# Gate-up weights of a mixture of experts: two quarter loads of 16 KB runs against one half load of 32 KB runs

## The chip, the cores and the metric

The kernel runs on one core of a Trainium2 chip. The metric is the device time of one execution in microseconds. The kernel before takes 1092.41 us, the median of three runs (1090.91 to 1093.58).

## The reference

One step of a decoder layer for 256 prompt tokens, with 16 meta tokens ahead of them, and 8 sample tokens. A mixer comes first; then a mixture of experts takes most of the time:

```
logits = xt @ w_router + b_router;  top_val, top_idx = lax.top_k(logits, 4);  gates = softmax(top_val)
for each expert e of 32, on the tokens that chose it:
    hgu  = x @ w_gu[e] + b_gu[e]                       # 1024 x 2048 weights, float32: 8.39 MB
    gate = minimum(hgu[:, :1024], 7);  up = clip(hgu[:, 1024:], -7, 7)
    act  = gate * sigmoid(1.702 * gate) * (up + 1)
    y   += (act @ w_down[e] + b_down[e]) * gate_of_token   # 1024 x 1024 weights: 4.19 MB
```

So each expert needs 12.58 MB of float32 weights from HBM, and 32 experts need 403 MB of the 432.68 MB that the whole kernel moves.

## The kernel before

The program is written engine by engine: each engine has one list of instructions, and semaphores join them. `sp` (SyncE) issues the weight loads, `pe` (TensorE) multiplies, `act` and `v` (ScalarE and VectorE) do what lies between. Nothing is reordered by a scheduler.

An *item* is one expert with 64 slots for its tokens. (If an expert had more than 64 tokens, further rounds of 32 items would follow; `more` is their number, and in this profile there are none.) TensorE does for item i:

1. `gate_up(i)`: eight steps k = 0 to 7, each with one slot of `gu_ring` as the moving operand (128 rows of w_gu, 2048 columns, four products of 512 columns). Each step adds 1 to `gu_used`. After k = 2, 4 and 6 stands one `scatter` of item i-2 (L1122, L1124), which brings its result back to the tokens. Items 28, 29 and 30 each have one scatter with bias products besides (L1119).
2. `way_back(i-1)` (L1157, L1159), then `gather()` for item i+1 (L1078), 56 small products.
3. `down(i-1)` (L1175): eight steps over `down_ring`; every second one adds 1 to `down_used`.
4. `turn(i)` (L1189, L1193): transposes of the hidden values.

`gu_ring` has 16 slots of 8 KB a partition: two items of eight slots, by parity. `down_ring` has eight slots of 4 KB a partition: one item, two halves. Of w_gu, `load_gu(e, parity, m)` brings a *chunk* m of 256 rows (0 to 3), 2.1 MB, into two slots: partition p gets rows 2p and 2p+1 of the chunk, one run of 16 KB. Each chunk has its own semaphore, `gu_landed[4 * parity + m]`, and TensorE waits for it at k = 0, 2, 4, 6 (L1142). `load_down` brings a half of w_down, also 2.1 MB in runs of 16 KB. `load_row` brings one slot of the first experts in runs of 8 KB.

All of these loads stand in one queue, in the order in which SyncE issues them, and SyncE waits before each until its slots are free: chunk m of item i after `gu_used` = 8i + 2m - 14 (step k = 2m + 1 of item i-2), half h of down(i) after `down_used` = 4i + 2h - 2. The order has three stages:

- *first stage*, to item 9: gate-up of i+2, then down of i;
- *middle stage*: chunks 2 and 3 of gate-up i+1, chunks 0 and 1 of gate-up i+2, then down of i;
- *last stage*, from down of 20 on: gate-up of i+1, then down of i. The last down weights (item 31) are loaded into free slots of `gu_ring` behind everything else.

The hidden index of the tokens' values has to be dealt to partitions as the rows of w_gu are. So the transposes and the gather read columns with a step of 2 (`(p r)` with r=2, L882, L989, L1079), and the router's weights are loaded likewise.

Of the kernel before, what the change touches and what calls it, by code (L numbers as in the profile page):

```python
# [51 lines left out]
def build(nc, x_prompt, x_sample, state_pool, state_conv, meta_tokens, g_mix, w_in, w_pool_grp, pool_scale,  # L52
          w_pool_up, w_conv, w_conv_out, w_o, g_ffn, w_router, b_router, w_gu, b_gu, w_down, b_down, g_final,
          y_prompt, y_sample, new_pool_prompt, new_conv_prompt, new_pool_sample, new_conv_sample):
    with ExitStack() as ctx:
# [108 lines left out]
        gffn_rows = low[0:CH, 9856:9856 + 2 * P]  # L164
# [143 lines left out]
        gu_landed = [sem(f"gu_landed{s}") for s in range(KT)]  # L308
        beside_landed = sem("beside_landed")
# [60 lines left out]
        def _(sp):  # L370
# [3 lines left out]
            def load_rows():  # L374
                for c in range(CH):
                    sp.dma_start(bgu_rows[E * c:E * c + E, :], b_gu[0, :, HALF * c:HALF * c + HALF]
                                 ).then_inc(rows_landed, 16)
                sp.dma_start(pool_rows, state_pool[0].rearrange("b r d -> (b r) d")).then_inc(rows_landed, 16)
                sp.dma_start(conv_rows, state_conv[0].rearrange("b r d -> (b r) d")).then_inc(rows_landed, 16)
                sp.dma_start(param_rows[0:4, :], pool_scale[0].rearrange("(k p) -> k p", p=P)).then_inc(rows_landed, 16)  # L380
                sp.dma_start(param_rows[4:16, :], w_conv[0].rearrange("w (k p) -> (w k) p", p=P)
                             ).then_inc(rows_landed, 16)
                sp.dma_start(gffn_rows, g_ffn[0].rearrange("(m c) -> m c", c=2 * P)).then_inc(rows_landed, 16)
# [28 lines left out]
            def load_row(e, parity, k):  # L412
                m, r = divmod(k, 2)
                sp.dma_start(gu_ring[:, KT * parity + k, :],
                             w_gu[0, e, 2 * P * m:2 * P * m + 2 * P, :].rearrange("(p r) n -> p r n", r=2)[:, r, :]
                             ).then_inc(gu_landed[CH * parity + m], 16)

            def load_gu(e, parity, m):
                src = w_gu[0, bass.ds(e, 1), 2 * P * m:2 * P * m + 2 * P, :].rearrange("a (p r) n -> (a p) (r n)", r=2)
                sp.dma_start(gu_ring[:, KT * parity + 2 * m:KT * parity + 2 * m + 2, :].rearrange("p s n -> p (s n)"),  # L420
                             src).then_inc(gu_landed[CH * parity + m], 16)
# [45 lines left out]
            def item_gu(i, e, parity, chunks=range(CH)):  # L467
                for m in chunks:
                    sp.wait_ge(gu_used, 8 * i + (2 * m - 14))
                    load_gu(e, parity, m)  # L470


            for k in range(2):
                sp.wait_ge(gu_used, k + 1)
                load_row(2, 0, k)
            item_gu(2, 2, 0, (1, 2, 3))
            item_gu(3, 3, 1)
# [15 lines left out]
            first, second = (0, 1), (2, 3)  # L493
# [18 lines left out]
            with sp.Fori(0, E // 2 - 2 - AHEAD - HALVED) as pair:  # L512
# [11 lines left out]
            with sp.If(more > 0):  # L524
                with sp.Fori(0, more) as r:
                    with sp.Fori(0, E // 2) as pair:
                        e0 = sp.snap(2 * pair)
                        e1 = sp.snap(2 * pair + 1)
                        e_before = sp.snap((2 * pair + (E - 1)) % E)
                        before = sp.snap(r * E + 2 * pair + (E - 1))  # L530
                        item_down(before, e_before)
                        item_gu(before + 1, e0, 0)
                        item_down(before + 1, e0)
                        item_gu(before + 2, e1, 1)
# [46 lines left out]
        def _(act):  # L581
# [67 lines left out]
            for b in range(NCHUNK // 2):  # L649
# [15 lines left out]
                if b == 4:  # L665
                    act.dma_start(wr[:].rearrange("p (m r) e -> p m r e", r=2),
                                  w_router[0].rearrange("(m p r) e -> p m r e", p=P, r=2)).then_inc(late_landed, 16)
# [187 lines left out]
        def _(pe):  # L855
# [23 lines left out]
            def turn_small_rows():  # L879
                pe.wait_ge(rows_landed, 144)  # L880
                nc.tensor.transpose(PS[:, 4, 8:24], param_rows, ident[0:16, 0:16])
                by_r = gffn_rows.rearrange("m (p r) -> m r p", r=2)  # L882
                for q in range(2):
                    last = nc.tensor.transpose(PS[:, 4, 24:32].rearrange("p (m r) -> p r m", r=2)[:, q, :], by_r[:, q, :],
                                               ident[0:CH, 0:CH])
# [101 lines left out]
            def by_row(rows, t, k):  # L987
                m, q = divmod(k, 2)
                return Y[0:rows, t, 2 * P * m:2 * P * m + 2 * P].rearrange("t (p r) -> t r p", r=2)[:, q, :]  # L989
# [85 lines left out]
            def gather_parts(k, parts, first, final, rows=None):  # L1075
                m, q = divmod(k, 2)
# [56 lines left out]
            def gate_up(i, u, landed, two_before, bias=None):  # L1133
# [62 lines left out]
            def item(i, u, landed, before=None, two_before=None, bias=None):  # L1196
                gate_up(i, u, landed, two_before, bias)
# [8 lines left out]
            gate_up(0, 0, 32, None)  # L1206
# [5 lines left out]
            item(1, 1, 32, 0)  # L1212
# [3 lines left out]
            with pe.Fori(0, more * (E // 2) + (E // 2 - 3)) as pair:  # L1216
                item(2 * pair + 2, 0, 16 * pair + 48, 2 * pair + 1, 2 * pair)
                item(2 * pair + 3, 1, 16 * pair + 48, 2 * pair + 2, 2 * pair + 1)
# [5 lines left out]
            landed = more * (8 * E) + (8 * E + 16)  # L1224
            pe.wait_ge(gt_kept, NT + 1)
            pe.wait_ge(late_landed, 80)
            item(from_end(4), 0, more * (8 * E) + 8 * E, from_end(5), from_end(6), bias=0)
            item(two_before, 1, more * (8 * E) + 8 * E, from_end(4), from_end(5), bias=1)
            item(before, 0, landed, two_before, from_end(4), bias=2)

            gate_up(last, 1, landed, two_before)
# [489 lines left out]
```

## Time and profile before

| | |
|---|---|
| median of three runs | 1092.41 us |
| profiled execution, device time | 1091.76 us |
| its span, first to last instruction | 1090.0 us |
| TensorE busy | 1050.4 us, 96% |
| VectorE / ScalarE busy | 458.7 / 173.6 us |
| moved by DMA | 432.68 MB, mean 397 GB/s |
| granted TensorE clock, mean | 0.998 of full |

TensorE and the DMA engines are both busy for nearly the whole span. A share of busy time cannot tell which of the two sets the end. The views to read are the transfer rate by stretch, and in each stage which wait TensorE ends last. The DMA share of a stretch can read slightly over 1, since packets of one engine overlap a little.

### The profile page before, as it was taken

The page shows a single profiled execution, that of the slowest core. Times are in us where ns is not written, and L with a number is a line of the kernel's source. Part 1 is how long each engine was busy: PE and PEld are TensorE (multiplying, and loading weights), DVE is VectorE, ACT ScalarE, POOL GpSimd, SP SyncE. Part 2 cuts the span into 40 slices and gives each one's busy share as a digit, 9 for nine tenths or more (in the row PEclk, how much of TensorE's full clock was granted, in tenths as well). Part 3 has the DMA queues.
Part 4 walks back from the last instruction along what each step waited for, and adds up shares of the span by engine and source line. Part 5 has one row for each costly group of instructions (what it writes and reads, how often), then busy time and mean ns, then how long its engine had stood idle before and what let it go on. Part 6 is the DMA issues. An engine that isn't in the chain of part 4 may idle for free.

```text
span 1090.0 us, 17300 instructions
## 1 busy us (share of the span) xinstructions
PE 1050.4 (96%) x7080; PEld 510.9 (47%) x7081; DVE 458.7 (42%) x776; ACT 173.6 (16%) x293; POOL 8.9 (1%) x21
## 2 busy tenths in 40 slices
PE   8999999999999999999999999999999999999995
PEld 7999975433344333444333333333433333343332
DVE  5677665333333333333333333333333333333344
ACT  5445533100000000000000000000000000000012
POOL 1000100000000000000000000000000000000000
PEclk9999999999999999999999999999999999999999
DMA  9972899999999999999999999999999999999993
GB/s 299 289 231 95 335 407 376 428 429 425 429 427 430 426 431 426 430 427 429 429 427 430 427 430 426 431 426 430 427 429 428 428 430 427 429 426 427 427 424 146
DMA packets 52482, 432.68 MB, mean 397 GB/s; under 512 B 4630, under 2 KB 21546, under 8 KB 26205
## 3 DMA queue, kind: packets, MB, share of 16 engines
q1 hardware_dynamic: 50959, 431.04, 95.2%
q10 hardware_dynamic: 1494, 1.22, 0.4%
q8 instruction: 22, 0.36, 0.1%
q14 instruction: 7, 0.06, 0.0%
HBM read 431.10 MB, written 1.39 MB: 397 GB/s over the span
## 4 chain that ended last, share of the span: by engine, by line
PE 61%; DMA 30%; DVE 4%; issue 4%; ACT 1%; SPq 1%; DVEq 0%; ACTq 0%
PE PS L1146 22%; DMA down_ring<-in_w_down_dram 19%; PE PS L1175 16%; DMA gu_ring<-in_w_gu_dram 11%; PE PS L914 9%; PE PS L1078 3%; PE PS L1122 2%; PE PS L945 2%; PE PS L1124 1%; PE PS L1189 1%; PE PS L1159 1%; PE PS L1157 1%; DVE pick_twice L1582 1%; PE PS L1193 1%; PE PS L865 0%
## 5 line engine op out<-in xcount | busy, mean ns | idle before, releaser
L1146 PE MATMUL PS<-gu_ring,XgT 128*64 128x512 f32 x2048 | 469.0, 599 | 4.0 <-DMA gu_ring<-in_w_gu_dram 4.0
L1146 PEld LDWEIGHTS PS<-gu_ring,XgT 128*64 128x64 f32 x2048 | 135.1, 136 | 267.2 <-issue 247.1
L1175 PE MATMUL PS<-down_ring,actT 128*64 128x512 f32 x984 | 219.7, 596 | 9.8 <-DMA down_ring<-in_w_down_dram 9.8
L1613 DVE TENSOR_TENSOR Y<-PS,Y 128x1024 f32<-128x1024 f32 (+1 forms) x96 | 117.0, 1220 | 255.1 <-PE PS L1124 255.1
L1175 PEld LDWEIGHTS PS<-down_ring,actT 128*64 128x64 f32 x984 | 67.3, 137 | 137.6 <-issue 118.4
L1644 DVE SCALAR_TENSOR_TENSOR y_low<-PS,slot_gate,y_high 128x512 fp32r<-128x512 f32 x31 | 23.3, 751 | 231.7 <-ACT y_high L801 231.7
L813 ACT ACTIVATE work<-PS 128x512 f32<-128x512 f32 x32 | 19.1, 597 | 456.3 <-PE PS L1146 456.3
L914 PE MATMUL PS<-h_high,win_high 128*128 128x264 f32 (+2 forms) x256 | 71.2, 287 | 0.0
L914 PE MATMUL PS<-h_high,win_low 128*128 128x264 f32 (+2 forms) x256 | 71.0, 286 | 0.0
L914 PE MATMUL PS<-h_low,win_high 128*128 128x264 f32 (+2 forms) x256 | 70.9, 286 | 0.0
L801 ACT ACTIVATE y_high<-PS,slot_gate 128x512 fp32r<-128x512 f32 x31 | 21.3, 687 | 258.4 <-PE PS L1175 258.4
L1078 PE MATMUL PS<-pick,XP 128*128 128x64 bf16 x1768 | 56.7, 193 | 0.0
L1078 PEld LDWEIGHTS PS<-pick,XP 128*128 128x128 bf16 x1768 | 56.2, 99 | 0.0
L1122 PEld LDWEIGHTS PS<-y_high,spread 64*128 64x128 f32 x186 | 17.3, 183 | 75.3 <-issue 74.5
L914 PEld LDWEIGHTS PS<-h_high,win_high 128*128 128x128 f32 x256 | 47.4, 189 | 0.4 <-issue 0.2
L914 PEld LDWEIGHTS PS<-h_low,win_high 128*128 128x128 f32 x256 | 47.4, 188 | 0.3 <-DVE h_low L1308 0.2
L914 PEld LDWEIGHTS PS<-h_high,win_low 128*128 128x128 f32 x256 | 47.3, 188 | 0.1
L1303 DVE TENSOR_TENSOR win_low<-gu_ring,win_high 128x2048 fp32r<-128x2048 f32 x15 | 34.4, 2292 | 30.2 <-ACT win_high L616 30.2
L1122 PE MATMUL PS<-y_high,spread 64*128 64x512 f32 x186 | 46.6, 498 | 0.0
L1550 DVE TENSOR_TENSOR XgT<-PS,params 128x512 f32<-128x512 f32 x31 | 21.4, 692 | 55.3 <-PE PS L1078 55.3
L1621 DVE TENSOR_TENSOR work<-PS,bias_gu 128x512 f32<-128x512 f32 x64 | 44.0, 687 | 1.2 <-PE PS L1193 0.6
L1124 PE MATMUL PS<-y_low,spread 64*128 64x512 f32 x186 | 36.7, 391 | 0.0
(235 smaller groups left out, 775.9 us busy)
## 6 DMA issues: line engine op xcount, KB each, us to landing
gu_ring<-in_w_gu_dram SPq DMA_DIRECT2D x119, 2048.0 KB, 28.2
down_ring<-in_w_down_dram SPq DMA_DIRECT2D x60, 2048.0 KB, 21.9
gu_ring<-in_w_gu_dram SPq DMA_DIRECT2D x18, 1024.0 KB, 9.4
gu_ring<-in_w_in_dram SPq DMA_DIRECT2D x16, 1024.0 KB, 9.5
gu_ring<-in_w_down_dram SPq DMA_DIRECT2D x4, 1024.0 KB, 27.9
down_ring<-in_w_down_dram SPq DMA_DIRECT2D x3, 1024.0 KB, 9.4
down_ring<-in_w_pool_up_dram SPq DMA_DIRECT2D x1, 2048.0 KB, 11.5
gu_ring<-in_w_conv_out_dram SPq DMA_DIRECT2D x2, 1024.0 KB, 6.2
```

Of the source, the lines that this page charges most:

```text
L914: return mm(PS[:, n % 4, 0:COLS - lo], w[:, k, P * (n % 2):P * (n % 2) + P], h[:, k, lo:COLS], start=first, stop=final)
L945: last = mm(PS[:, 4 + n % 4, 0:TOK], of(w, k, m), x[:, k, :], start=(k == 0 and part == 0), stop=(k == CH - 1 and part == 2))
L1078: last = mm(rows if rows is not None else PS[:, 5, SLOTS * k:SLOTS * k + SLOTS], XP[:, part, 2 * P * m:2 * P * m + 2 * P].rearrange("t (p ...
L1122: mm(PS[:, bank + h, :], way[rows, t, :], y_high[rows, :], start=not bias, stop=False)
L1124: last = mm(PS[:, bank + h, :], way[rows, t, :], y_low[rows, :], start=False, stop=True)
L1146: last = mm(PS[SLOTS * h:SLOTS * h + SLOTS, b, :], XgT[:, k, :], w[:, D * b + HALF * h:D * b + HALF * h + HALF], start=(k == 0), stop=(k = ...
L1175: last = mm(PS[SLOTS * h:SLOTS * h + SLOTS, bank, :], acts[:, f % 4, f // 4, :], rows[:, f, HALF * h:HALF * h + HALF], start=(f == 0), sto ...
L1303: tt(win_low[:, b % WIN_SLOTS, :], gu_ring[:, b % WIN_SLOTS, :], win_high[:, b % 2, :].bitcast(F32), ALU.subtract).then_inc(win_ready, 1)
L1550: tt(XgT[:], PS[:, 5, :].rearrange("p (k s) -> p k s", k=KT), g_ffn_cols.unsqueeze(2).to_broadcast([P, KT, SLOTS]), ALU.mult).then_inc(xg_ ...
L1613: tt(Y[rows, t, :].rearrange("p (h n) -> p h n", h=2), PS[rows, bank:bank + 2, :], Y[rows, t, :].rearrange("p (h n) -> p h n", h=2), ALU.a ...
L1621: tt(hgu[:, HALF * b:HALF * b + HALF].rearrange("p (c s) -> p c s", s=SLOTS), PS[:, 2 + b, :].rearrange("p (c s) -> p c s", s=SLOTS), bias ...
L1644: stt(y_low[:], PS[:, bank, :], gate[:], y_high[:].bitcast(F32), ALU.mult, ALU.subtract).then_inc(low_ready, 1)
```

## The change

The gate-up weights of experts 4 to 29, and the second half of expert 3, are loaded by halves of 512 rows, 4.2 MB each: partition p gets rows 4p to 4p+3 of the half, one run of 32 KB. There are 53 such half loads in place of 106 chunk loads. Experts 30 and 31, all but the last half of experts 2 and 3, stay in chunks: a chunk is now two of the four rows of each partition, a run of 16 KB with a step of 32 KB between partitions. TensorE waits twice in an item instead of four times (k = 0 and k = 4), SyncE issues a half when all four slots of it are free (`gu_used` = 8i + 4h - 12). The first waits of items 2 and 3 have semaphores of their own. Everything that is dealt as the rows are has a step of 4 instead of 2. The order of the loads by item stays; the last two items are written out behind the test for further rounds.

```diff
+            def load_gu(e, parity, m, signal):
+                h, q = divmod(m, 2)
+                src = w_gu[0, bass.ds(e, 1), HALF * h:HALF * h + HALF, :].rearrange("a (p q r) n -> (a p) q (r n)", q=2, r=2)
                 sp.dma_start(gu_ring[:, KT * parity + 2 * m:KT * parity + 2 * m + 2, :].rearrange("p s n -> p (s n)"),
-                             src).then_inc(gu_landed[CH * parity + m], 16)
+                             src[:, q, :]).then_inc(signal, 16)
+
+            def load_half(e, parity, h):
+                src = w_gu[0, bass.ds(e, 1), HALF * h:HALF * h + HALF, :].rearrange("a (p r) n -> (a p) (r n)", r=CH)
+                at = KT * parity + CH * h
+                sp.dma_start(gu_ring[:, at:at + CH, :].rearrange("p s n -> p (s n)"), src
+                             ).then_inc(half_landed[2 * parity + h], 16)
...
-            def item_gu(i, e, parity, chunks=range(CH)):
-                for m in chunks:
-                    sp.wait_ge(gu_used, 8 * i + (2 * m - 14))
-                    load_gu(e, parity, m)
+            def item_gu(i, e, parity, halves=range(2)):
+                for h in halves:
+                    sp.wait_ge(gu_used, 8 * i + (4 * h - 12))
+                    load_half(e, parity, h)
...
-            item_gu(2, 2, 0, (1, 2, 3))
-            item_gu(3, 3, 1)
+            for m, signal in ((1, half_landed[0]), (2, third_chunk), (3, half_landed[1])):
+                item_chunk(2, 2, 0, m, signal)
+            for m, signal in ((0, fourth_chunk), (1, half_landed[2])):
+                item_chunk(3, 3, 1, m, signal)
+            item_gu(3, 3, 1, (1,))
...
-            with sp.Fori(0, E // 2 - 2 - AHEAD - HALVED) as pair:
+            with sp.Fori(0, E // 2 - 3 - AHEAD - HALVED) as pair:
...
+            for u in range(2):
+                for m in range(CH):
+                    item_chunk(more * E + (E - 2 + u), E - 2 + u, u, m, gu_landed[CH * u + m])
+                item_down(more * E + (E - 3 + u), E - 3 + u)
...
             def gather_parts(k, parts, first, final, rows=None):
-                m, q = divmod(k, 2)
+                m, q = divmod(k, CH)
                 for n, (part, t) in enumerate(parts):
                     last = mm(rows if rows is not None else PS[:, 5, SLOTS * k:SLOTS * k + SLOTS],
-                              XP[:, part, 2 * P * m:2 * P * m + 2 * P].rearrange("t (p r) -> t r p", r=2)[:, q, :],
+                              XP[:, part, HALF * m:HALF * m + HALF].rearrange("t (p r) -> t r p", r=CH)[:, q, :],
...
-                    if k % 2 == 0:
-                        by_row = 16 if k == 0 and u == 0 and two_before is not None else 0
-                        pe.wait_ge(gu_landed[CH * u + k // 2], landed + by_row)
+                    if chunks and k % 2 == 0:
+                        pe.wait_ge(gu_landed[CH * u + k // 2], landed)
+                    elif not chunks and k % CH == 0:
+                        if k == 0:
+                            pe.wait_ge(*((fourth_chunk, 16) if u else (third_rows, 32)))
+                        elif u == 0:
+                            pe.wait_ge(third_chunk, 16)
+                        pe.wait_ge(half_landed[2 * u + k // CH], landed)
...
-            item(before, 0, landed, two_before, from_end(4), bias=2)
-
-            gate_up(last, 1, landed, two_before)
+            item(before, 0, 48, two_before, from_end(4), bias=2, chunks=True)
+
+            gate_up(last, 1, 48, two_before, chunks=True)
```

What moves on TensorE is shown at the gate-up of an odd item inside the loop over pairs of items, where the last stage has its waits. One step k is four products here, at L1146 (after: L1174); in the trace each product is two records, so a step is eight. Before:

```order
L1146 MATMUL PS<-gu_ring,XgT 64x512 [waits gu_landed4,xg_ready]
L1146 MATMUL PS<-gu_ring,XgT 64x512 x7
L1146 MATMUL PS<-gu_ring,XgT 64x512 [waits gu_landed5]
L1146 MATMUL PS<-gu_ring,XgT 64x512 x3
L1130 ISA [waits low_ready]
L1122 MATMUL PS<-y_high,spread 128x512 [waits added]
L1122 MATMUL PS<-y_high,spread 128x512
L1124 MATMUL PS<-y_low,spread 128x512 x2
L1146 MATMUL PS<-gu_ring,XgT 64x512 x4
L1146 MATMUL PS<-gu_ring,XgT 64x512 [waits gu_landed6]
```

After, at the same place:

```order
L1174 MATMUL PS<-gu_ring,XgT 64x512 [waits half_landed2,fourth_chunk,xg_ready]
L1174 MATMUL PS<-gu_ring,XgT 64x512 x11
L1153 ISA [waits low_ready]
L1145 MATMUL PS<-y_high,spread 128x512 [waits added]
L1145 MATMUL PS<-y_high,spread 128x512
L1147 MATMUL PS<-y_low,spread 128x512 x2
L1174 MATMUL PS<-gu_ring,XgT 64x512 x4
L1174 MATMUL PS<-gu_ring,XgT 64x512 [waits half_landed3]
```

The products and their order are the same; the wait ahead of k = 2 is gone, what it waited for now stands ahead of k = 0, and the wait ahead of k = 4 asks for chunks 2 and 3 together.

On SyncE, the loop of the last stage (L512; after: L530), one item of it. Before:

```order
L420 ISA [waits gu_used]
L420 DMA gu_ring<-in_w_gu_dram 128x4096
L469 REGISTER_ALU
L420 ISA [waits gu_used]
L420 DMA gu_ring<-in_w_gu_dram 128x4096
L464 ISA
L427 ISA [waits down_used]
L427 DMA down_ring<-in_w_down_dram 128x4096
L427 ISA [waits down_used]
L427 DMA down_ring<-in_w_down_dram 128x4096
```

These are chunks 2 and 3 of an item's gate-up load and both halves of its down load. After:

```order
L431 ISA [waits gu_used]
L431 DMA gu_ring<-in_w_gu_dram 128x8192
L480 REGISTER_ALU
L431 ISA [waits gu_used]
L431 DMA gu_ring<-in_w_gu_dram 128x8192
L475 ISA
L438 ISA [waits down_used]
L438 DMA down_ring<-in_w_down_dram 128x4096
L438 ISA [waits down_used]
L438 DMA down_ring<-in_w_down_dram 128x4096
```

Here the two gate-up rows are the whole item: four chunk loads of 4096 values a partition have become two loads of 8192 values, ahead of the same two down loads.

## Rows read from the trace of the kernel before

**Rows 1.** Page, part 2: 40 slices of the span (27.25 us each).
```profile
PE   8999999999999999999999999999999999999995
DMA  9972899999999999999999999999999999999993
GB/s 299 289 231 95 335 407 376 428 429 425 429 427 430 426 431 426 430 427 429 429 427 430 427 430 426 431 426 430 427 429 428 428 430 427 429 426 427 427 424 146
```

**Rows 2.** Busy time by window: length; PE, PEld, DVE, ACT, POOL; clock; DMA; GB/s.
```profile
131.00:143.00 12.00, 12.00 (x119) 9.14 (x118) 6.33 (x26) 3.76 (x7) 4.07 (x6) 1.00 1.00 410
134.00:154.00 20.00, 20.00 (x145) 15.12 (x145) 13.88 (x26) 4.39 (x13) 2.41 (x4) 1.00 1.02 421
570.00:780.00 210.00, 199.71 (x1305) 79.55 (x1303) 73.70 (x120) 17.95 (x36) 0.00 (x0) 1.00 1.01 429
```

**Rows 3.** TensorE in time, item 3 (first stage): start, length, line, idle before it.
```profile
243.66 5.37 PE L1146 MATMUL PS<-gu_ring,XgT 128*64 128x512 f32 x24
...
249.63 3.65 PE L1146 MATMUL PS<-gu_ring,XgT 128*64 128x512 f32 x16
...
271.26 5.37 PE L1146 MATMUL PS<-gu_ring,XgT 128*64 128x512 f32 x24
```

**Rows 4.** TensorE in time, middle stage, two items.
```profile
630.07 3.65 PE L1175 MATMUL PS<-down_ring,actT 128*64 128x512 f32 x16 [1.24 <-DMA down_ring<-in_w_down_dram]
...
659.44 3.65 PE L1175 MATMUL PS<-down_ring,actT 128*64 128x512 f32 x16 [1.24 <-DMA down_ring<-in_w_down_dram]
...
664.18 5.37 PE L1146 MATMUL PS<-gu_ring,XgT 128*64 128x512 f32 x24
```

**Rows 5.** TensorE in time, last stage, the gate-up of item 26 and the next.
```profile
894.36 1.94 PE L1146 MATMUL PS<-gu_ring,XgT 128*64 128x512 f32 x8 [0.25 <-DMA gu_ring<-in_w_gu_dram]
...
899.25 1.94 PE L1146 MATMUL PS<-gu_ring,XgT 128*64 128x512 f32 x8 [0.43 <-DMA gu_ring<-in_w_gu_dram]
...
904.15 1.94 PE L1146 MATMUL PS<-gu_ring,XgT 128*64 128x512 f32 x8 [0.44 <-DMA gu_ring<-in_w_gu_dram]
...
919.82 3.65 PE L1146 MATMUL PS<-gu_ring,XgT 128*64 128x512 f32 x16
```

**Rows 6.** The chain that ended last, two transfers of it: start, length.
```profile
950.16 37.13 DMA gu_ring<-in_w_gu_dram
...
1010.73 41.73 DMA gu_ring<-in_w_gu_dram
```

**Rows 7.** TensorE in time, items 29 to 31 and the last down.
```profile
989.21 1.98 PE L1119 MATMUL PS<-Y,work 32*128 32x512 f32 x4
...
1009.16 5.37 PE L1146 MATMUL PS<-gu_ring,XgT 128*64 128x512 f32 x24
...
1019.37 1.94 PE L1146 MATMUL PS<-gu_ring,XgT 128*64 128x512 f32 x8
1021.60 1.94 PE L1146 MATMUL PS<-gu_ring,XgT 128*64 128x512 f32 x8 [0.28 <-DMA gu_ring<-in_w_gu_dram]
...
1039.17 5.37 PE L1146 MATMUL PS<-gu_ring,XgT 128*64 128x512 f32 x24
...
1052.51 1.94 PE L1146 MATMUL PS<-gu_ring,XgT 128*64 128x512 f32 x8 [0.28 <-DMA gu_ring<-in_w_gu_dram]
```

**Rows 8.** SyncE's load issues in time: start of the first, length, count.
```profile
160.12 18.10 SPq L414 DMA_DIRECT2D gu_ring<-in_w_gu_dram  x7
181.32 24.29 SPq L420 DMA_DIRECT2D gu_ring<-in_w_gu_dram  x7
```

**Rows 9.** Weight loads of TensorE by form: count, busy us, mean ns.
```profile
L1078 PEld LDWEIGHTS PS<-pick,XP 128*128 128x128 bf16 x1768 | 56.2, 99 | 0.0
L1189 PEld LDWEIGHTS PS<-ident,work 128*128 128x128 f32 x128 | 18.0, 210 | 24.3 <-issue 24.3
L999 PEld LDWEIGHTS PS<-ident,Y 128*128 128x128 f32 x16 | 2.5, 204 | 0.5 <-issue 0.3
L1012 PEld LDWEIGHTS PS<-mask_small,ones 128*128 128x128 bf16 x6 | 0.4, 110 | 0.5 <-DVE mask_small L1490 0.5
```

More of the change, by code:

```diff
@@ L308, in build @@
         gu_landed = [sem(f"gu_landed{s}") for s in range(KT)]
+        half_landed = [sem(f"half_landed{s}") for s in range(4)]
+        third_rows = sem("third_rows")
+        third_chunk = sem("third_chunk")
+        fourth_chunk = sem("fourth_chunk")
         beside_landed = sem("beside_landed")
@@ L382, in load_rows @@
                              ).then_inc(rows_landed, 16)
-                sp.dma_start(gffn_rows, g_ffn[0].rearrange("(m c) -> m c", c=2 * P)).then_inc(rows_landed, 16)
+                sp.dma_start(gffn_rows, g_ffn[0].rearrange("(m c) -> m c", c=HALF)).then_inc(rows_landed, 16)
             for b in range(NCHUNK // 2):
@@ L492, in _ @@
                 item_down(i + 1, e1)
-            first, second = (0, 1), (2, 3)
+            first, second = (0,), (1,)
             i = 2 * AHEAD + 1
@@ L881, in turn_small_rows @@
                 nc.tensor.transpose(PS[:, 4, 8:24], param_rows, ident[0:16, 0:16])
[L882 to L885, printed above, removed]
+                by_r = gffn_rows.rearrange("m (p r) -> m r p", r=CH)
+                for q in range(CH):
+                    last = nc.tensor.transpose(PS[:, 4, 24:32].rearrange("p (m r) -> p r m", r=CH)[:, q, :], by_r[:, q, :],
+                                               ident[0:2, 0:2])
                 last.then_inc(rows_turned, 1)
@@ L1131, in scatter_item, with gate_up @@
                 scatter(t, bias=bias)
-            def gate_up(i, u, landed, two_before, bias=None):
+            def gate_up(i, u, landed, two_before, bias=None, chunks=False):
                 by_halves = type(i) is int and i == 0
@@ L1194, in turn, with item @@
                 last.then_inc(up_turned, 1)
-            def item(i, u, landed, before=None, two_before=None, bias=None):
-                gate_up(i, u, landed, two_before, bias)
+            def item(i, u, landed, before=None, two_before=None, bias=None, chunks=False):
+                gate_up(i, u, landed, two_before, bias, chunks)
                 if before is not None:
@@ L1204, in item @@
                 turn(i)
-            gate_up(0, 0, 32, None)
+            gate_up(0, 0, 32, None, chunks=True)
             turn_gates()
@@ L1211, in _ @@
             turn(0)
-            item(1, 1, 32, 0)
+            item(1, 1, 32, 0, chunks=True)
             pe.wait_ge(next_landed, 16)
@@ L1216, in _ @@
             with pe.Fori(0, more * (E // 2) + (E // 2 - 3)) as pair:
-                item(2 * pair + 2, 0, 16 * pair + 48, 2 * pair + 1, 2 * pair)
-                item(2 * pair + 3, 1, 16 * pair + 48, 2 * pair + 2, 2 * pair + 1)
+                item(2 * pair + 2, 0, 16 * pair + 16, 2 * pair + 1, 2 * pair)
+                item(2 * pair + 3, 1, 16 * pair + 16, 2 * pair + 2, 2 * pair + 1)
             def from_end(n):
```

43 lines of the change are left out of this document (22 added, 21 removed).

## The prediction, made before the changed kernel was run

> **What bounds the kernel now.** I read the page's 40 slices first. From the eighth slice on the rate stands at 424 to 431 GB/s in nearly every slice, while TensorE is also 9 tenths busy or more [rows 1]. So both are candidates, and the question is which one sets the pace. The pace of each follows from two other views. One item of TensorE's work without a wait takes 271.26 - 243.66 = 27.6 us [rows 3]. One item of weights is 12.58 MB, and at 428.5 GB/s that is 29.36 us, or 4.89 us for each of six loads of 2.1 MB. So the transfers are slower by 1.76 us an item. The first stage runs at 27.6 us only because loads had run ahead; the lead is then used up. In the middle stage TensorE ends the same wait of 1.24 us every 659.44 - 630.07 = 29.37 us [rows 4], which is the pace of the transfers. In the last stage the place of the wait changes: it is now the gate-up, which waits chunk by chunk, 0.25, 0.43 and 0.44 us, with the waits at 894.36, 899.25 and 904.15, again 4.9 us apart [rows 5]. The end then hangs on the chain's transfers, chunk 2 of item 29, which lands at 950.16 + 37.13 = 987.29, and chunk 3 of item 31, which lands at 1010.73 + 41.73 = 1052.46; TensorE takes its step k = 6 at 1052.51 and never waits for a weight again [rows 6, 7]. Two things decide therefore: how long the queue needs to its last gate-up loads, and how late TensorE stands behind them.
>
> **What larger runs give the transfers.** The trace has two sizes of run at full queue. In the stage of the 8 KB row loads the rate is 421 GB/s over 20 us, and 410 over a 12 us piece of it; with runs of 16 KB it is 429 (I use 428.5, between 428 and 429) [rows 1, 2]. A run of 8 KB on one of 16 engines takes 8192 x 16 / 421 = 311.3 ns, a run of 16 KB 16384 x 16 / 428.5 = 611.8 ns. Two of the first are 622.6, so 10.8 ns went with each run saved. If that is a fixed cost of a run, the next doubling saves the same again: 32 KB in 2 x 611.8 - 10.8 = 1212.8 ns. A half load is eight such runs on each engine, so it saves 8 x 10.8 = 86 ns of 9.79 us. There are 53 of them: 4.6 us. This goes into the end in full, since the queue is full from item 4 on and TensorE is waiting for it in the middle and the last stage. Bounds: by the 410 piece the saving of a run is 2 x 319.7 - 611.8 = 27.6 ns, or 11.7 us in all; on the other side nothing in this trace shows a 32 KB run, and if its wider step slows the transfers down to the 421 of the 8 KB stage, a half load takes 0.17 us more and the sum is a loss of 9.2 us. I take 4.6, since the 20 us row is the steadier one.
>
> A rule of the Trainium skill speaks against the gain: "DMA: Bandwidth & Descriptors", section "Why small descriptors are slow", has a fixed cost of about 3 cycles a packet and finds joining worth it only at 256 bytes or less. At the 850 MHz of its section "Where 436 GB/s comes from" that is 3.5 ns, and 53 x 8 x 3.5 gives 1.5 us where the rows give 4.6. The second of these sections also puts the ceiling at 435 GB/s, which would cap the gain at 53 x 9.79 x (1 - 428.5/435.2) = 8.0 us. The trace shows 10.8 ns a run, three times the rule, so I keep the rows' value.
>
> **What waiting by halves costs.** In an unhindered item, step k = 3 begins 249.63 - 243.66 = 5.97 us after the gate-up's start and a step takes 3.58 / 2 = 1.79 us, so k = 4 stands at 7.76 us, and from there to the next gate-up are 19.84 us [rows 3].
> - *First stage:* loads are far ahead, the waits fall on nothing.
> - *Middle stage:* the gate-up after the wait at 659.44 starts at 664.18 [rows 4]. Chunks 2 and 3 of it stand in the queue right behind that down half and land 2 x 4.89 later, at 669.2; k = 4 is at 671.9. So the half is there 2.7 us early, where the single chunk 2 was 7.6 us early. Cost nothing; without that cover it would be the part over 2.7 us.
> - *Last stage:* here there is no cover. The queue holds the gate-up after the down, chunks land 4.89 us apart, and TensorE follows them just in time. It now may begin k = 4 only when chunk 3 has landed, where before it began k = 6 then. The two steps k = 4, 5 and a scatter, some 4.2 us, move behind that landing. One item then takes, from the landing, 19.84 + 7.76 = 27.6 us, still under 29.2, so the delay doesn't grow from item to item; it is paid once, at the end.
>
> The end, step by step. Chunk 3 of item 29 landed at 987.29 + 4.89 = 992.2; call D the time gained by the queue. Item 29 begins k = 4 at 992.2 - D. To the start of item 30's gate-up are 19.84 us and 1.91 for the bias products of item 29 (their record is 1.98 long with its overlap) [rows 7]: 1013.95 - D, against 1009.16 before. Items 30 and 31 have chunks as before. Item 30 took 1039.17 - 1009.16 = 30.01 us, of which 1021.60 - (1019.37 + 1.79) = 0.44 was its wait; without it 29.57, so item 31 starts at 1043.5 - D. Its k = 6 is 7.76 + 1.79 + 0.73 + 1.79 = 12.07 us after the start: 1055.6 - D. Before it was at 1052.51. The landing of chunk 3 of item 31, 1052.46 - D, is 3.1 us earlier than that and doesn't bind. Net: 3.1 - D = 3.1 - 4.6 = **1.5 us less**. The queue is never empty meanwhile: the first down half is used, and its successor issued, some 8.5 + 3.2 + 3.5 = 15 us after the landing of the item's last gate-up half; behind that landing stood six loads, 29.4 us, so 14 us are still to move. Of the 3.1 us, 1.3 are what TensorE waited in items 30 and 31 and no longer does, already taken in.
>
> **The other edits.** *Issue by halves.* The first half of an item waits for step 3 instead of 1, 4.2 us longer. It would cost only if the queue ran dry. The tightest place is the half load of item 3: it goes out at 181.32 + 24.29 = 205.6 less one issue, about 205.3, where its first chunk went at about 202. The queue got 12.6 MB from about 178 on [rows 8], 29.4 us of moving, so it has work until 207.4. Two microseconds cover the start of a transfer; I take nothing, at worst 1 us. In the last stage SyncE waits for `down_used`, and the gate-up slots are free by then. *Loading `more` before the last two items* stands behind a down load with 20 us of work in the queue: nothing. *Fewer waits and loads* on TensorE and SyncE: neither queue is short of time; nothing. *A step of 4 in the gather and the transposes:* weight loads of float32 take 210 ns at a step of 4 (L1189) and 204 at a step of 2 (L999); those of the gather, bfloat16, 99 ns at a step of 2, no more than the 110 of a contiguous one (L1012) [rows 9]. The 56 loads hide beside the products; nothing, and at the other end 6 ns each, 0.3 us an item if it all showed, twice behind item 29's landing, 0.7 us. *Two more transposes of g_ffn's rows*, some 0.3 us each at most and before the queue is full, may count 0.3 us once; inside the error.
>
> **The sum.** Profiled execution: 1091.8 us, span 1090.0; less 1.5 gives 1090.3. It lies 0.6 under the median of the runs. On the median: 1092.4 - 1.5 = **1090.9 us**. A measurement of this kernel tells about 0.3% (3.3 us) from no change, and 1.5 us is within that.
>
> **Rivals.**
> 1. *The long run brings nothing* (it is moved as two of 16 KB, or the 10.8 ns are of the smaller loads, which also came twice as many, not of the run). D = 0; the wait by halves alone remains: 1092.4 + 3.1 = 1095.5. For it: no row shows a run of 32 KB. Against: the step from 8 to 16 KB did raise the rate. Chance 17%.
> 2. *Slower: the 32 KB step between partitions slows reading.* The engines then read places twice as far apart. Its place is each half load; it decides from the point where a half saves less than 3.1 / 53 = 58 ns. At 421 GB/s D = -9.2 and the time is 1092.4 + 3.1 + 9.2 = 1104.7. Against it: the row loads of 8 KB had a step twice their length as well and ran at 421. Chance 11%. [...]
> 3. *Faster: a run costs more than I take.* At 27.6 ns D is 11.7 and the time 1092.4 + 3.1 - 11.7 = 1083.8; half way, at 19.2 ns, D is 8.1 and the time 1087.4. For it: the 410 row. Against: the longer window. Chance 18%.
> 4. *The step of 4 slows the gather* so far that TensorE sets the end alone. From item 3's gate-up at 243.66 to item 31's at 1039.17 are 28 items in 795.5 us [rows 3, 7]; unhindered, with three bias parts, they would take 28 x 27.6 + 5.7 = 778.5. So it decides from 0.6 us an item, 11 ns on each of 56 loads; at 1 us an item the time is 1092.4 + 28 - 17 = 1103.4. The float32 pair of 204 and 210 ns speaks against it [rows 9]. Chance 4%.
>
> **Chances and range.** My own case has 50%, with 1088.8 to 1093.5 as its own range. Faster by over 0.3%: a tenth of it and nearly all of rival 3, 21%. Slower: a twentieth of it, half of rival 1 (3.1 us stands at the bound), all of 2 and 4, 25%. Within: 54%. The range reaches from half way of rival 3 to a little above rival 1: 1086.5 to 1096.5.
>
> **What would show it.** In the changed profile the rate from slice 10 on should read 430 to 432 instead of 428.5, with 53 x 128 = 6784 fewer packets of weights. The middle stage's period should be 29.2 us, with the wait still at the down's second half. From item 23 to 29 TensorE should wait at k = 4 alone, about 1.6 us an item, and items 30 and 31 should show no wait for a chunk. If the rate is 428 and the waits are as said, rival 1 holds; if it is under 428, rival 2; if the gather takes over 2 us, rival 4. I am wrong in the mechanism if the last stage has no wait at k = 4, or if TensorE waits there in the middle stage.

## The result: 3.7 us slower

| kernel | median | runs | lowest to highest |
|---|---|---|---|
| before | 1092.41 us | 5 | 1089.78 to 1093.58 |
| after | 1096.08 us | 5 | 1095.20 to 1096.59 |

The ratio is 1.0038 [1.0028, 1.0049]: slower by over 0.3%. I had forecast 1.5 us less; the time lies in the range, 0.4 us under its upper end, but on the other side. The profiled execution of after took 1096.08 us with a span of 1094.3, so 4.3 us of span are to be found against 1090.0.

**The profile after.** The slices of the page, to be laid beside [rows 1]:

```profile
PE   8999999999999999999999999999999999999995
...
PEclk9999998999999999999999999999999999999999
...
GB/s 295 284 233 98 333 395 330 437 401 429 434 428 431 430 430 432 426 434 428 435 426 432 426 431 431 431 431 429 431 430 431 430 437 430 430 428 425 428 423 111
```

The steady rate is up, as forecast: 431 in most slices where it was 428. But slice 7 moved 330 GB/s where it was 376, slice 9 401 where it was 429, and in slice 7 the granted clock is below full. The loss is early. By window (columns as in [rows 2]), after and then before:

```profile
160.00:174.00 14.00, 13.31 (x116) 11.62 (x114) 10.78 (x36) 8.75 (x19) 0.00 (x0) 1.00 1.01 414
174.00:182.00 8.00, 8.00 (x27) 4.18 (x28) 5.38 (x22) 3.10 (x5) 0.00 (x0) 0.57 0.45 160
182.00:224.00 42.00, 42.00 (x302) 18.13 (x300) 10.49 (x23) 5.68 (x11) 0.00 (x0) 1.00 0.99 416
224.00:236.00 12.00, 12.00 (x60) 3.80 (x56) 4.12 (x5) 0.00 (x0) 0.00 (x0) 1.00 0.94 380
```

```profile
160.00:174.00 14.00, 13.12 (x123) 11.59 (x122) 10.73 (x36) 8.92 (x17) 0.00 (x0) 1.00 1.01 420
174.00:182.00 8.00, 8.00 (x41) 2.79 (x42) 5.05 (x22) 2.43 (x4) 0.00 (x0) 1.00 0.80 277
182.00:224.00 42.00, 42.00 (x304) 17.81 (x302) 12.98 (x23) 5.67 (x11) 0.00 (x0) 1.00 1.01 425
224.00:236.00 12.00, 11.68 (x109) 5.31 (x107) 4.69 (x9) 1.15 (x3) 0.00 (x0) 1.00 1.00 424
```

Length times the difference of the rates, over 428.5 GB/s, is the time that the queue lost: 0.2, 2.2, 0.9 and 1.2 us, 4.5 together. In the second window the clock stood at 0.57: it was at its lower level, 1.2 GHz, for some 7 of the 8 us. TensorE's rows there, after and then before:

```profile
172.87 4.00 PE L1120 MATMUL PS<-before_spread,Y 128*128 128x64 f32 x16
176.80 16.53 PE L1174 MATMUL PS<-gu_ring,XgT 128*64 128x512 f32 x64
...
196.73 3.65 PE L1174 MATMUL PS<-gu_ring,XgT 128*64 128x512 f32 x16
```

```profile
172.17 2.10 PE L1097 MATMUL PS<-before_spread,Y 128*128 128x64 f32 x16
174.20 13.95 PE L1146 MATMUL PS<-gu_ring,XgT 128*64 128x512 f32 x64
```

The 16 products that gather item 0 from `Y` took 4.00 us instead of 2.10, and item 0's gate-up 16.53 instead of 13.95. Before them stands why (weight loads: count, busy, mean ns), after and then before:

```profile
L1101 PEld LDWEIGHTS PS<-pick,XP 128*128 128x128 bf16 x1768 | 63.8, 119 | 0.0
...
L1120 PEld LDWEIGHTS PS<-before_spread,Y 128*128 128x128 f32 x16 | 3.8, 328 | 0.4 <-DVE before_spread L1573 0.4
...
L1022 PEld LDWEIGHTS PS<-ident,Y 128*128 128x128 f32 x16 | 2.5, 205 | 0.5 <-issue 0.3
```

```profile
L1097 PEld LDWEIGHTS PS<-before_spread,Y x16: 193/196/197, 172.2 to 173.9; 128*128 128x128 f32 x16
```

With a step of 4, a float32 weight load of these products takes 328 ns instead of 196, and a bfloat16 one 119 instead of 99 [rows 9]. The transposes at L1022, float32 with the same step of 4, take 205: they did not slow down. Late products free the slots of gate-up weights late, so SyncE's next loads go out late; its issues, to be laid beside [rows 8]:

```profile
160.83 22.57 SPq L418 DMA_DIRECT2D gu_ring<-in_w_gu_dram  x7
186.51 17.68 SPq L425 DMA_DIRECT2D gu_ring<-in_w_gu_dram  x5
210.73 0.33 SPq L431 DMA_DIRECT2D gu_ring<-in_w_gu_dram  x1
217.24 0.33 SPq L406 DMA_DIRECT2D down_ring<-in_w_down_dram  x1
220.67 0.33 SPq L438 DMA_DIRECT2D down_ring<-in_w_down_dram  x1
229.67 8.82 SPq L431 DMA_DIRECT2D gu_ring<-in_w_gu_dram  x2
```

The row that starts at 186.51 started at 181.32 before; the first half of item 4 goes out at 229.67, 9 us behind the down half at 220.67, and the queue ran short there (the last window). In the middle stage TensorE at first takes items without a wait, 27.82 us each, where [rows 4] have 29.37 with one; from 691.15 on it waits for the down's second half, three times and 29.2 us apart:

```profile
611.25 5.37 PE L1174 MATMUL PS<-gu_ring,XgT 128*64 128x512 f32 x24
...
639.08 5.37 PE L1174 MATMUL PS<-gu_ring,XgT 128*64 128x512 f32 x24
...
666.90 3.65 PE L1174 MATMUL PS<-gu_ring,XgT 128*64 128x512 f32 x16
...
691.15 3.65 PE L1203 MATMUL PS<-down_ring,actT 128*64 128x512 f32 x16 [0.95 <-DMA down_ring<-in_w_down_dram]
...
720.37 3.65 PE L1203 MATMUL PS<-down_ring,actT 128*64 128x512 f32 x16 [1.18 <-DMA down_ring<-in_w_down_dram]
```

An unhindered item of before is 27.6 [rows 3]; the gather's 56 slower loads show as 0.2 us of it. The last stage, to be laid beside [rows 5, 7]:

```profile
847.03 1.94 PE L1174 MATMUL PS<-gu_ring,XgT 128*64 128x512 f32 x8 [1.24 <-DMA gu_ring<-in_w_gu_dram]
...
876.15 1.94 PE L1174 MATMUL PS<-gu_ring,XgT 128*64 128x512 f32 x8 [1.08 <-DMA gu_ring<-in_w_gu_dram]
...
905.46 1.94 PE L1174 MATMUL PS<-gu_ring,XgT 128*64 128x512 f32 x8 [1.26 <-DMA gu_ring<-in_w_gu_dram]
...
993.02 1.94 PE L1174 MATMUL PS<-gu_ring,XgT 128*64 128x512 f32 x8 [0.68 <-DMA gu_ring<-in_w_gu_dram]
...
1044.78 5.37 PE L1174 MATMUL PS<-gu_ring,XgT 128*64 128x512 f32 x24
...
1055.00 3.65 PE L1174 MATMUL PS<-gu_ring,XgT 128*64 128x512 f32 x16
```

Each wait for gate-up weights is at k = 4, as forecast, and items 30 and 31 have none. The period from item 24 to item 29 is (993.02 - 847.03) / 5 = 29.20 us. The last row holds k = 5 and 6 of item 31, so k = 6 is at 1055.00 + 1.79 = 1056.79, 4.28 us behind the 1052.51 of [rows 7], which is the whole difference of the spans. The sum of 4.3 thus is: k = 4 of item 29 comes 0.8 behind the 992.2 of before; from there the wait by halves costs 3.1, and two gathers at 0.2, 0.4. The 0.8 is a gain by the longer runs and an early loss. From 300 to 949 us after moved 279.48 MB and before 278.12, which is 3.2 us for 44 half loads, or 72 ns each and 3.8 us for 53; the early loss is then 4.6 as the remainder, and 4.5 by the windows above. Counted in bytes, though, after is 2.18 MB or 5.1 us behind at 300 us and still 1.9 us at 949 us, so these two terms are known to about 1 us only.

### The profile page after: what moved, and what is told of

The parts are those of the page before. It is cut to its first block, busy times and chain, and to the rows that moved or that the text cites. A ratio compares the mean times of both kernels' runs of the same rounds, so it can differ in the third digit from the quotient of the medians.

```text
span 1094.3 us, 17096 instructions
## 1 busy us (share of the span) xinstructions
PE 1059.9 (97%) x7083; PEld 522.9 (48%) x7083; DVE 458.8 (42%) x776; ACT 173.9 (16%) x293; POOL 9.0 (1%) x21
## 2 busy tenths in 40 slices
DMA packets 44590, 432.68 MB, mean 395 GB/s; under 512 B 3268, under 2 KB 20436, under 8 KB 25097
## 4 chain that ended last, share of the span: by engine, by line
PE 73%; DMA 18%; DVE 4%; issue 4%; ACT 1%; SPq 0%; DVEq 0%; ACTq 0%
PE PS L1174 28%; PE PS L1203 18%; DMA gu_ring<-in_w_gu_dram 10%; PE PS L937 9%; DMA down_ring<-in_w_down_dram 7%; PE PS L1101 4%; PE PS L1145 3%; PE PS L968 2%; PE PS L1147 2%; PE PS L1217 1%; PE PS L1187 1%; PE PS L1185 1%; DVE pick_twice L1610 1%; PE PS L1221 1%; PE PS L888 0%
## 5 line engine op out<-in xcount | busy, mean ns | idle before, releaser
L1174 PE MATMUL PS<-gu_ring,XgT 128*64 128x512 f32 x2048 | 470.1, 601 | 5.3 <-DMA gu_ring<-in_w_gu_dram 5.3
L1174 PEld LDWEIGHTS PS<-gu_ring,XgT 128*64 128x64 f32 x2048 | 136.3, 137 | 268.5 <-issue 258.4
L1101 PE MATMUL PS<-pick,XP 128*128 128x64 bf16 x1768 | 63.9, 197 | 0.0
L1101 PEld LDWEIGHTS PS<-pick,XP 128*128 128x128 bf16 x1768 | 63.8, 119 | 0.0
```

Source lines behind the costliest of these rows:

```text
L1174: last = mm(PS[SLOTS * h:SLOTS * h + SLOTS, b, :], XgT[:, k, :], w[:, D * b + HALF * h:D * b + HALF * h + HALF], start=(k == 0), stop=(k = ...
```

## The experiments

The theory after the result (A): the loss is early, from the step of 4 in the products that gather item 0 and in the gather, and late, from the wait by halves; the run of 32 KB itself gains. The rivals are told in the expectations. Each kernel was timed in five rounds, in three groups at different times (e1 to e4, e5 to e8, e9 and e10), each with its own runs of the kernel before. The kernel after was in none of them: where an experiment is compared with it, the two differences from before are compared.

**e1: before, with only the dealing changed to four.** Loads stay in chunks, waits as before.

```diff
-                m, r = divmod(k, 2)
+                h, r = divmod(k, CH)
...
-                src = w_gu[0, bass.ds(e, 1), 2 * P * m:2 * P * m + 2 * P, :].rearrange("a (p r) n -> (a p) (r n)", r=2)
+                h, q = divmod(m, 2)
+                src = w_gu[0, bass.ds(e, 1), HALF * h:HALF * h + HALF, :].rearrange("a (p q r) n -> (a p) q (r n)", q=2, r=2)
```

> The kernel before with only the dealing of rows changed to four a partition; loads and waits stay by chunks of 16 KB runs, now 32 KB apart. Theory A (the fallen clock and the late queue come from the dealing): the 16 products with the tokens' values at step 4 take 4.0 us instead of 2.0 and TensorE's clock falls to half for about 7 us around 175 us, the queue stands 3.2 us later from item 2 on, the gather takes 0.2 us more an item; time 3.2 + 0.5 = 3.7 us over before, 1096.1. Theory B (the coarse waits and issues are the whole loss, the clock is an accident of the run): no fall of the clock that lasts, 1092.4. Theory C (the slower gather, 0.23 us in each of 28 items, goes into the time in full): clock held, 1092.4 + 6.4 = 1098.8.

Measured: 1094.4 us (8 runs, before 1091.76), ratio 1.0025 [1.0014, 1.0035], +2.6. TensorE in time:

```profile
173.07 3.75 PE L1098 MATMUL PS<-before_spread,Y 128*128 128x64 f32 x16
176.75 15.65 PE L1147 MATMUL PS<-gu_ring,XgT 128*64 128x512 f32 x64
...
1054.94 1.94 PE L1147 MATMUL PS<-gu_ring,XgT 128*64 128x512 f32 x8 [0.69 <-DMA gu_ring<-in_w_gu_dram]
```

The step alone brings the slow products, a lower clock and a later k = 6 of item 31, by 2.43 us; of the 3.7 us that I had expected, 2.6 are there. The rate stays at 428: chunks with a step of 32 KB between partitions are moved as fast as before. The clock fell twice here. It is 0.79 in 174 to 182 us, and before that (by window):

```profile
170.00:174.00 4.00, 3.78 (x50) 3.57 (x50) 2.67 (x11) 1.59 (x3) 0.00 (x0) 0.57 1.01 424
```

A mean of 0.57 is 3.4 of 4 us at the lower level. The slow products start only at 173.07, so this first fall came ahead of them; the window from 171 to 172 us already reads 0.50. The slow products can't have brought that one about.

**e2: after, dealing by two again;** a half load is two runs of 16 KB a partition. It keeps the waits and issues by halves.

```diff
-                src = w_gu[0, bass.ds(e, 1), HALF * h:HALF * h + HALF, :].rearrange("a (p r) n -> (a p) (r n)", r=CH)
+                src = w_gu[0, bass.ds(e, 1), HALF * h:HALF * h + HALF, :].rearrange("a (q p r) n -> p (a q) (r n)", q=2, r=2)
```

> The changed kernel with the dealing put back to two rows a partition: the half loads remain one load of 4.2 MB with waits and issue by halves, but of two runs of 16 KB a partition. Theory A: clock held at 175 us, rate 428.5 GB/s as before, the queue 1.2 us late from item 4's first half, waits at k = 4 in the last stage, 3.1 us at the end, 0.3 us back from fewer loads: 1092.4 + 4.0 = 1096.4. Theory B: the same 1096 or more, since here stands the whole loss and no gain of the runs (1092.4 + 3.7 + 3.9 = 1100.0). Theory C: 1092.4.

Measured: 1096.98 us (6 runs, two of them far out, at 1099.44 and 1101.89), 1.0057 [1.004, 1.0074], +5.2.

```profile
173.11 2.10 PE L1119 MATMUL PS<-before_spread,Y 128*128 128x64 f32 x16
175.13 13.95 PE L1173 MATMUL PS<-gu_ring,XgT 128*64 128x512 f32 x64
...
994.16 1.94 PE L1173 MATMUL PS<-gu_ring,XgT 128*64 128x512 f32 x8 [1.42 <-DMA gu_ring<-in_w_gu_dram]
...
1055.70 3.65 PE L1173 MATMUL PS<-gu_ring,XgT 128*64 128x512 f32 x16
```

Products at 2.10 and gate-up 0 at 13.95 are back in this execution, whose clock reads 1.00 in every window from 160 to 1039 us. Yet four of the six runs had a mean clock of 0.993 to 0.996, where each of the 15 runs of before in this group had 0.997 or 0.998. So a lower clock also comes without slow products; at what time it fell in those runs is not known. From k = 4 of item 29 to k = 6 of item 31 are 1057.49 - 994.16 = 63.33 us, where I had forecast 1055.6 - 992.2 = 63.4: the price of the halves at the end is as worked out. The rest, 2.0 us at item 29, is early: with loads issued by halves, the rate in 182 to 224 us is 419 and in 224 to 236 us 408, which is 1.0 us. The other 1.0 us was missing at 182 us already (51.34 MB moved, before: 51.75). The profiled executions of e5 and e7 to e10, which also deal item 0 by two, had moved 51.4 to 51.7 MB by then, so part of it is the spread between executions.

**e3: after, with more products that fill TensorE's wait ahead of item 0** (`FILL = (8, 3)` for `(2, 3)`), to hold the clock.

> The changed kernel with 8 filler products instead of 2 ahead of the 16 products at step 4. Theory A: if the clock falls because TensorE does too little there, the fillers hold it at 2.4 GHz; item 0's gate-up takes 13.9 us again instead of 16.5, for 6 x 0.21 = 1.3 us of fillers; the queue gets back 3.2 - 1.3 = 1.9 us: 1094.2. If the 16 products still take 4.0 us, their weight loads are slow by the step and not by the clock. Theory B: the clock is beside the point, 1096 to 1097.

Measured: 1096.28 us (5 runs), 1.004 [1.0027, 1.0053]. In two runs the mean clock was 0.998, at 1094.71 and 1095.54 us, in three 0.996, at 1096.28 to 1096.74. The profiled one is the first:

```profile
173.85 3.73 PE L1120 MATMUL PS<-before_spread,Y 128*128 128x64 f32 x16
177.51 13.95 PE L1174 MATMUL PS<-gu_ring,XgT 128*64 128x512 f32 x64
```

Gate-up 0 is back at 13.95 and the products are not: they are slow at the full clock too, so they don't need a fallen clock to be slow, and what the clock costs is a second loss. As a remedy it fails: three of five runs still had the lower mean clock, and the products start 1 us later.

**e4: after, with item 4 loaded by chunks** and the items 2 and 3 written out ahead of TensorE's loop over pairs, to close the gap at 229.67.

```diff
-            item_gu(4, 4, 0)
+            for m in range(CH):
+                item_chunk(4, 4, 0, m, half_landed[m // 2])
```

> The changed kernel with item 4 loaded by chunks of 16 KB runs, each issued as its two slots come free; its waits stay by halves. Theory A: the gap in the transfers at 228 us (281 GB/s in 4 us) closes, 1.2 us less: 1094.9. Theory B (the coarse waits, not the issues): 1096.1.

Measured: 1094.97 us (7 runs), 1.0031 [1.0019, 1.0042]; three runs at clock 0.997 took 1093.06 to 1093.80, three at 0.995 took 1095.84 to 1096.88. The seventh had 0.996 and took 1094.97. So the lower clock goes with 2 to 3 us here. In e1 it does not: its two runs at 0.994 took 1093.77 and 1094.48, its three at 0.997 took 1093.59 to 1094.47. The profiled execution, at full clock:

```profile
172.27 3.95 PE L1121 MATMUL PS<-before_spread,Y 128*128 128x64 f32 x16
...
989.99 1.94 PE L1175 MATMUL PS<-gu_ring,XgT 128*64 128x512 f32 x8 [0.68 <-DMA gu_ring<-in_w_gu_dram]
...
1051.99 3.65 PE L1175 MATMUL PS<-gu_ring,XgT 128*64 128x512 f32 x16
```

In 224 to 236 us the rate is 431 (after: 380); a smaller gap of 1 us comes one item later (365 GB/s in 256 to 260 us). Item 29's k = 4 is 2.2 us ahead of before's 992.2, and the end still comes 1.3 later: the late price is untouched.

**e5: after, with item 0 dealt by two.** Rows, router and transposes of item 0 go by two, the gather from item 1 on by four; a second set of `g_ffn`'s rows is loaded for it. In this kernel and in e7 the router's weights are scaled by `g_ffn` as dealt by four, so that tokens choose somewhat other experts; in e9 and e10 they are scaled as dealt by two.

```diff
-                m, q = divmod(k, CH)
+                r = 2 if rows is not None else CH
+                m, q = divmod(k, r)
...
+                if e == 0:
+                    m, r = divmod(k, 2)
```

> The changed kernel, but item 0's rows, the router's and all transposes and products ahead of item 0 stay dealt by two; only the gathers from item 1 on have a step of 4. Theory A (slow weight loads of the 16 float32 products at step 4, 4.0 us instead of 2.0, and with them the fall of the clock, make the queue late): the 16 products take 2.0 us again, the clock holds, item 0's gate-up takes 13.9 us, the queue stands 3.2 us earlier at item 2 than in the changed kernel; its time is 1.0 us over the kernel before. Rival B (the clock falls for another reason, such as the place of the program in time): the clock still falls in most runs, 3 to 4 us over before. Rival C (the slow gathers cost in full, 28 x 0.23 us): also 3 us or more over before with the clock held.

Measured: 1092.71 us (11 runs, before 1091.9), 1.0012 [1.0003, 1.0022], +0.8. The products take 2.10 us and the clock is 0.997 or 0.998 in every run. Over before it is 0.8 us where after is 3.7: 2.9 us of after's loss, give or take 1.5 by the two intervals, came from the step of four in what stands ahead of item 1: item 0's products and the transposes before them together.

**e6: after, with items 22 to 31 loaded and awaited by chunks;** a second loop on SyncE and on TensorE.

```diff
+            with pe.Fori(0, more * (E // 2) + 3) as pair:
+                item(2 * pair + 22, 0, 16 * pair + 48, 2 * pair + 21, 2 * pair + 20, chunks=True)
+                item(2 * pair + 23, 1, 16 * pair + 48, 2 * pair + 22, 2 * pair + 21, chunks=True)
```

> The changed kernel with items 22 to 31 loaded and waited for by chunks of 16 KB runs; halves of 32 KB runs up to item 21. Theory A (4.2 us of TensorE's work stand behind the last half's landing, 3.1 us at the end): k = 6 of item 31 waits for its own chunk again and stands 3.6 us earlier than in the changed kernel (1.2 us of the runs' gain given up, the rest of the wait taken back), so about 0.1 to 0.4 us over before. Rival: the wait by halves is hidden and its loss lies elsewhere; the time goes up by the 1.2 us of gain given up, to 5 us over before.

Measured: 1094.18 us (10 runs), 1.002 [1.0011, 1.003], +2.3: 1.4 less than after's 3.7, yet 2 us more than expected. Most of that goes with the clock: of ten runs five had a clock of 0.994, at 1094.12 to 1095.12, and two 0.996, at 1092.88 and 1095.24; the three at 0.997 and 0.998 took 1091.10 to 1093.26, around the 1091.9 of before.

**e7: all three remedies, and e8: the same with dealing by two and runs of 16 KB.** The pair measures the long run by itself: 35 half loads of 32 KB runs against the same 35 with two runs of 16 KB.

> All three remedies together: item 0 dealt by two, item 4 by chunks, items 22 to 31 by chunks; 35 half loads of 32 KB runs stay. Theory A: clock held, queue 35 x 0.073 = 2.6 us ahead of before less 1.0 for the gap that moves on to item 5 or 6: 1.6 us under the kernel before, 1090.2 where before is 1091.8. Rival (something else of the change costs): not under before.

> As the last one, but everything dealt by two and each half load made of two runs of 16 KB a partition: halves without longer runs, with early and late chunks. Theory A: the rate stays 428.5 GB/s, nothing is gained but 35 x 0.01 us, the gap of 1.0 us stays: 0.7 us over before, and 2.3 us over the last kernel, which is what the runs of 32 KB alone bring here. Rival (the gain is of fewer loads and semaphores, not of the runs): the same time as the last kernel.

Measured: e7 1090.42 us (11 runs), 0.9986 [0.9977, 0.9995]; e8 1092.77 (11 runs), 1.0013 [1.0004, 1.0022]. The difference is 2.35 us, or 67 ns a half load, although e8's gather is the faster one. The run of 32 KB is a gain, by most of what the rows of before gave (86). The two kernels differ in the scaling of the router too; e9 below, scaled as e8 is, has the gain as well, 1.8 us under its before where e8 is 0.9 over.

**e9: e7 with the router scaled as dealt by two, and e10: the same without the late chunks.**

> The kernel with all three remedies, in which the router's weights are scaled by g_ffn dealt by two, as they are; in its forerunner they were scaled by the values dealt by four. Nothing is added in time. Theory A: 1.5 us under the kernel before, as the forerunner. Rival (the forerunner's gain came from its other choice of tokens for the experts): not under before.

> The same without the late chunks: item 0 dealt by two, item 4 by chunks, halves of 32 KB runs up to item 29. Theory A: the wait by halves at the end is back for 3.1 us, 18 more half loads give 1.3 us, and the extra loop of the late chunks with its 1.5 us on the queue is gone: between the forerunners with (1090.4) and with item 0 alone (1092.7), at 0.4 us over before. Rival (waits by halves at the end are hidden): 1.2 us or more under the kernel with all three remedies.

Measured: e9 1089.79 us (11 runs, before 1091.62), 0.9983 [0.9974, 0.9992]; e10 1092.71 (11 runs), 1.0011 [1.0002, 1.002]. The difference of 2.9 us is more than the 1.9 that I had expected, and it is a net one: e10 has 18 more half loads. Item 29 and item 31 of e10, then of e9:

```profile
989.18 1.94 PE L1189 MATMUL PS<-gu_ring,XgT 128*64 128x512 f32 x8 [1.06 <-DMA gu_ring<-in_w_gu_dram]
...
1051.15 3.65 PE L1189 MATMUL PS<-gu_ring,XgT 128*64 128x512 f32 x16
```

```profile
985.52 1.94 PE L1194 MATMUL PS<-gu_ring,XgT 128*64 128x512 f32 x8 [0.20 <-DMA gu_ring<-in_w_gu_dram]
...
1048.55 3.65 PE L1194 MATMUL PS<-gu_ring,XgT 128*64 128x512 f32 x16
```

k = 6 of item 31 stands at 1052.94 in e10 and 1050.34 in e9, which is 2.2 ahead of before and all of e9's shorter span (1087.8 to 1090.0). At 985.52 e9 waits for chunk 2 of item 29; chunk 3 lands 4.89 us later, at 990.4, which is 1.2 us behind the same weights in e10. So e10's queue was 1.2 us ahead and its end 2.6 us behind: waiting by halves takes 3.8 us of span there. The 1.5 us that the expectation of e10 puts down to an extra loop don't show: e7, where SyncE and TensorE enter their second loop, moved 428 GB/s in 780 to 830 us, where before has 427. e9 beats both kernels: it is 1.8 us under before, and after is 3.7 over it.

## Why the prediction was wrong

The stretch from item 29 to the end, in one table (the last column is what follows the landing, free of what the queue did before; where the load comes in chunks, it is the landing of chunk 3, at which k = 4 could begin if TensorE waited by halves):

| kernel | gather's step | item 29's last gate-up weights | k = 6 of item 31 | between |
|---|---|---|---|---|
| before | 2 | 992.2 | 1052.51 | 60.3 |
| e9 | 4 | 990.4 | 1050.34 | 59.9 |
| forecast | 2 | 992.2 - D | 1055.6 - D | 63.4 |
| e2 | 2 | 994.16 | 1057.49 | 63.33 |
| after | 4 | 993.02 | 1056.79 | 63.77 |
| e4 | 4 | 989.99 | 1053.78 | 63.79 |
| e10 | 4 | 989.18 | 1052.94 | 63.76 |

- **The step that failed is "A step of 4 in the gather and the transposes: ... nothing".** It took the float32 transposes (210 and 204 ns) to stand for all float32 weight loads, and left out that item 0 is gathered by 16 products from `Y` itself, whose weight loads take 328 ns at the step of 4 (196 before). Their 1.9 us are on the path of item 0. In the profiled execution of after the clock fell while they ran, and its some 7 us at the lower level cost 2.6 us of item 0's gate-up; e1 shows that the products alone don't explain the fall. The queue passes both on, since SyncE refills the slots that item 0 frees. e5 takes 2.9 us away by undoing the step ahead of item 1. Rival 4 named the kind of mechanism, with 4%, but in the gather of each item. There a load takes 20 ns more, above the 11 that it had asked for, yet the item only 0.2 us more, under its 0.6, where 56 loads of 20 ns would be 1.1: most of it is hidden behind the products. The one place where it decides was in neither.
- **"Issue by halves ... nothing, at worst 1 us" was too low, and looked at the wrong load.** Not item 3's half is the tightest, but item 4's first: issued at 229.67, it cost 1.2 us in the windows of after; in e2, without the slow products, the two windows from 182 to 236 us lose 0.6 and 0.4 us. With item 4 by chunks, e10 has 425 GB/s in both, as before.
- **What waiting by halves costs, 3.1 us, was right** in place and size: 63.33 us for 63.4 in e2, 3.0 over the 60.3 of before. Between e9 and e10, both with the gather's step of 4, it is 3.8. The gather's other end, "twice behind item 29's landing, 0.7 us", measures 0.4.
- **What larger runs give was right in kind and a little too large.** By the bytes moved, a half load saves 72 ns instead of 86, some 9 ns a run instead of 10.8, and 53 of them 3.8 us instead of 4.6. e7 and e8 give 67 ns, from timed runs. The Trainium skill, "DMA: Bandwidth & Descriptors", section "Why small descriptors are slow", has about 3 cycles a packet; my estimate from it, 1.5 us, is under half of what the runs show.
- **The middle stage was right in its end and wrong in its start.** I forecast a period of 29.2 us with the wait at the down's second half. That is what its last three waits show (691.15, 720.37 and 749.58, 29.2 us apart). Up to the first of them TensorE ran at 27.82 us without a wait, where before has such waits from 404.95 on. The lead of the loads is used up more slowly: the items are longer than I took (27.82 for 27.6), and the queue's are shorter. e1, with the longer items and the rate of before, has its first such wait at 661.88, so both have a part. The first k = 4 wait is at item 24, and those of items 24 to 27 are 1.1 to 1.3 us, that of item 29 0.68, where I said 1.6; e2, whose gather keeps the step of 2, has 0.69 at item 23 and 1.4 to 1.6 after it. What counts for the end is the queue's 29.2 us an item, which is right.
- **The packets:** 400 us of the middle hold 7936 packets instead of 11767, at 431 GB/s instead of 428; the whole span has 44590 instead of 52482, of which 6784 are the weights'.

The sum: forecast -1.5; 0.8 less gained by the runs; 4.6 lost early where I had none; 0.4 for the gathers. That is +4.3, as the spans have it. The range held only by luck: rival 1, which is not what happened, reached as far. One sum of the chances is off by a point: the parts named for slower add up to 26%, not 25.

What stays open: why the same step leaves the transposes alone and slows the products' weight loads; no run takes these apart. What makes the clock fall stays open too: it fell ahead of the slow products in e1 and was low in runs of e2, which has none. How much of the 4.6 us is the clock's alone is known only roughly: runs of one kernel differ with it by 1.5 to 3 us in e3 and e4, and not at all in e1.

## What to carry to other kernels

A load that is laid out otherwise in memory changes the access pattern of everything that is dealt to match it: cost each reader by its own row, and a row of another kind of instruction (a transpose for a product) is no bound for it. Larger transfers gain by the run, but what waits for them waits for more; keep the long loads where the queue has a lead, and small ones where the consumer follows each landing, at the start and at the end of the stream. A loss ahead of a queue that is full from there on is not caught up by the engine's later slack: e1 was 1.46 MB behind before at 300 us and 1.49 MB, or 3.5 us, at 949 us.

## What the hardware showed that I had not expected

- A weight load's time depends on the element step and on the kind of operation: float32 for a product 196 ns at a step of 2 and 328 at 4; for a transpose 204 and 205; bfloat16 99 and 119.
- The granted clock can fall in the midst of TensorE's work. In the profiled execution of after it went to its lower level at about 175 us, while the slow products ran, for some 7 us; in e1 twice for 3.4 us, the first time ahead of those products. The mean clock was 0.996 or less in all five runs of after, in five of eight of e1, three of five of e3, four of seven of e4 and seven of ten of e6, all of which have the slow products. It was so in two of the 68 runs of before and in one of the 55 of e5 and e7 to e10, which deal item 0 by two, but in four of six of e2, which deals everything by two. So the slow products go with a lower clock, and are not needed for it; that they bring it about is not shown.
